# The first block and the value weights of a gated-attention and short-conv layer: low parts on VectorE alone, some weights' high parts on ScalarE

## The chip, the core and the metric

The kernel runs on one core of a Trainium2 chip. The metric is the device time of one launch in microseconds (us). A run is compared by that time; the profile is of one execution and has a span of its own, which is a little shorter than the time of the launch.

## What is computed

The reference is one layer of a streaming encoder trunk, on x of 4096 tokens by 1024 channels in float32:

```
n = RMSNorm(h) * norm_w
z = n @ W_in                 # q, k, v, gate, a_low, and four conv groups, 3600 columns
GLA : 4 heads, chunk-causal gated linear attention with a low-rank decay, RMSNorm per head, SiLU gate
conv: Bg * conv3(Cg * u), SiLU gate
h = h + W_out [GLA ; conv]
h = h + sigmoid(h W_g + b_g) * (p W_ple)
out = RMSNorm(h)
```

All that matters here is the head of it: the norm of the first 512 tokens, and the products of these tokens with the columns of k and a_low (272 of them), of v (512), of q (256) and of the gate (512).

## The kernel before

**Split operands.** TensorE reads float32 operands in the form fp32r. To keep float32 accuracy each operand is split into a high part (the value rounded to fp32r, by ScalarE or GpSimd) and a low part (value minus high part, by VectorE or GpSimd), and each product is three matmuls: high by high, high by low weights, low tokens by high weights (L815, L816 and L823 in `big_tile`). A low part cannot be made before its high part.

**Blocks.** The 4096 tokens are eight blocks of 512. The program has three phases: GLA (eight blocks), a fast matrix product for the conv part and the output projection (`STEPS` of seven products), and the gate phase. For one block, `raw` holds the tokens (eight tiles of 128 channels by 512 tokens), `XH` and `XL` their normalised high and low parts. A GLA block has 14 tiles of 24 matmuls each: in block 0 four ka tiles (128 tokens by 272 columns), four v tiles (128 tokens by 512 columns), two q tiles and four gate tiles.

**The head of the program.** Block 0 is loaded by SyncE's queue in four transfers of 512 KB, then two quarters of the ka weights (`early_ka`), the constants, and the four value tiles (`early_v`). GpSimd's own queue loads the other two quarters of ka into `stage` (L596). ScalarE squares the tokens (L1215), VectorE sums the squares (L1531), TensorE sums over partitions (L846), ScalarE takes the root (L1224). Then VectorE works through the block in two halves of 256 tokens (L1957): reciprocal (L1959), eight normalising instructions (L1964), then low parts k = 3 to 7 (L1970); the low parts k = 0 to 2 of each half are GpSimd's (`lo_of_block_0`, L601). ScalarE makes the high parts of a half as the normalised tiles come (L1500, L1507), and between the halves the high parts of value tiles 1 to 3 (L1503). After the second half VectorE makes the low parts of value tiles 2 and 3 (L1974) and a small one of `wup` (L1978).

**GpSimd's list** (L606) is written out by hand: high and low parts of the four quarters of the ka weights (L636, L638), the three low parts of half A, the loads of the first two of the six q and gate weight tiles (L612, L613), both parts of value tile 0, the three low parts of half B, the low part of value tile 1, then both parts of the six q and gate tiles, and after that twelve `prep_pair` calls that make the weights of the second phase and store them to memory.

**TensorE's waits in block 0.** The first ka tile waits for all four quarters of ka (`ka_tile`, L871), and per k for the high and the low part of half A. The second needs nothing more. The third (tokens 256 to 383) waits per k for half B, the fourth for nothing more. The v tiles wait for all four value tiles (L879, L880), the q and gate tiles for theirs (`weights`, L842). Then, in order: the statistics of block 1 half way through the second q tile (L850, L851; they need `x_split`, L1536), and the decay's sums.

**Block 1's tokens.** SyncE stores the normalised block 0 to memory (L407) once all of it is normalised, and loads block 1 into the same `raw` (L402) once the low parts are done and the store has landed.

Of the kernel before, what the change touches and what calls it, by code (L numbers as in the profile page):

```python
# [28 lines left out]
KT = D_MODEL // P  # L29
HEADS, DK, DV = 4, 64, 128  # L30
QK, RANK, CHUNK = HEADS * DK, 16, 64
KA = QK + RANK
# [2 lines left out]
PLE_K = 2  # L35
UP = 96
EPS = 1e-6
FIRST_LO = 3
V_BY_DVE = 2
HALF_A, HALF_B = slice(0, TB // 2), slice(TB // 2, TB)  # L40
BIG = D_MODEL * 4
ROW = TB * 4
# [1 line left out]
F32 = mybir.dt.float32  # L44
# [52 lines left out]
def build(nc, xb, pb, w_ka, w_in, w_out, w_gate, w_ple, w_up, b_alpha, vectors, masks,  # L97
          out, y_scratch, h_scratch, n_scratch, w_scratch, g_scratch):
    with ExitStack() as ctx:
# [3 lines left out]
        def sem(name):  # L103
            return ctx.enter_context(nc.semaphore(name))
# [107 lines left out]
        stage_loaded = [sem(f"stage_loaded{i}") for i in range(2)]  # L212
        early_loaded = [sem(f"early_loaded{i}") for i in range(6)]
        w_hi = sem("w_hi")
        v_hi = sem("v_hi")
        v_lo = sem("v_lo")
        w_ready = sem("w_ready")
# [121 lines left out]
        def is_first(b):  # L339
            return isinstance(b, int) and b == 0  # L340
# [238 lines left out]
        def _(pool):  # L579
# [15 lines left out]
                src = source(n)  # L595
                pool.dma_start(stage[:, n % 2, 0:src.shape[1]], src).then_inc(stage_loaded[n % 2], 16)  # L596

            def lo_of_block_0(half, hi_done, lo_done):
                for k in range(FIRST_LO):
                    pool.wait_ge(hi_done, k + 1)  # L600
                    pool.tensor_tensor(XL[:, k, half], raw[:, k, half], XH[:, k, half].bitcast(F32),  # L601
                                       ALU.subtract).then_inc(lo_done, 1)

            load(0)
            load(1)
            for n in range(N_W):  # L606
                if W_Q < n < N_W - 1:
                    load(n + 1)
                if n == W_V:
                    lo_of_block_0(HALF_A, first_hi, first_lo)  # L610
                    pool.wait_ge(w_ready, 2)
                    load(W_Q)  # L612
                    load(W_Q + 1)  # L613
                if n == W_V + 1:
                    lo_of_block_0(HALF_B, x_hi, x_lo)
                if W_Q - V_BY_DVE <= n < W_Q:
                    continue
                if 2 <= n < W_Q:
                    source_tile = early_ka[n - 2] if n < W_V else early_v[n - W_V]
                    pool.wait_ge(early_loaded[n - 2], 16)  # L620
                else:
                    source_tile = stage[:, n % 2]
                    pool.wait_ge(stage_loaded[n % 2], 16 * (n // 2 + 1 if n < 2 else n // 2 - 2))
                if n < W_V:
                    hi, lo = KAH[:, 2 * n:2 * n + 2], KAL[:, 2 * n:2 * n + 2]
                    src = source_tile[:, 0:2 * KA].rearrange("p (k c) -> p k c", k=2)
                elif n < W_Q:
                    hi, lo = VH[:, n - W_V], VL[:, n - W_V]
                    src = source_tile.rearrange("p (k c) -> p k c", k=KT)
                else:  # L630
                    hi, lo = QG[:, n - W_Q, 0], QG[:, n - W_Q, 1]
                    src = source_tile.rearrange("p (k c) -> p k c", k=KT)
                if W_V < n < W_Q:
                    pool.wait_ge(v_hi, n - W_V)
                else:
                    pool.tensor_scalar(hi, src, 1.0, 0.0, ALU.mult, ALU.add).then_inc(w_hi, 1)  # L636
                    pool.wait_ge(w_hi, n + 1 if n <= W_V else n - 2)
                pool.tensor_tensor(lo, src, hi.bitcast(F32), ALU.subtract).then_inc(w_ready, 1)  # L638


# [158 lines left out]
        def _(pe):  # L799
            def big_tile(phase, b, i, acc_ap, products, after=None, waits=None):  # L800

                step = 8 * phase + b
                last = i == TILES[phase] - 1
                ahead = phase == GLA and is_first(b) and i == 0
                first = i == (1 if phase == GATE else 2 if phase == GLA and is_first(b) else 0)
                for k in range(KT):
                    hh, lh, hl = products(k)  # L810
                    if ahead:
                        pe.wait_ge(first_hi, k + 1)
                    elif first:
# [53 lines left out]
                return ps[MAIN[i % 3]]  # L867

            def ka_tile(b, t, after=None):
                if is_first(b):  # L870
                    pe.wait_ge(w_ready, W_V)  # L871
                tok = slice(t * P, t * P + P)
                big_tile(GLA, b, ka_place(b, t), main_bank(b, ka_place(b, t))[:, 0:KA],
                         lambda k: ((XH[:, k, tok], KAH[:, k]), (XH[:, k, tok], KAL[:, k]),
                                    (XL[:, k, tok], KAH[:, k])), after)
# [317 lines left out]
        def _(act):  # L1193
# [292 lines left out]
            def out_rms(b):  # L1486
# [2 lines left out]
                nc.scalar.activation(R_out[:], ps[STAT][:], ACT.Sqrt, bias=eps[:], scale=1.0 / D_MODEL).then_inc(  # L1489
                    out_root, 1)  # L1490

            act.wait_ge(memsets, 5)
            nc.scalar.activation(warm[:], eps[:], ACT.Sqrt)
            x_squares(0, range(KT))
            x_rms(0)
            act.wait_ge(consts_loaded, 64)
            nc.scalar.activation(suffix[:], mask[:, 0:P], ACT.Copy).then_inc(suffix_ready, 1)
            for k in range(KT):
                act.wait_ge(first_n, k + 1)
                nc.scalar.activation(XH[:, k, HALF_A], raw[:, k, HALF_A], ACT.Copy).then_inc(first_hi, 1)  # L1500
            for i in range(1, 4):
                act.wait_ge(early_loaded[2 + i], 16)
                nc.scalar.activation(VH[:, i], early_v[i].rearrange("p (k c) -> p k c", k=KT), ACT.Copy).then_inc(  # L1503
                    v_hi, 1)
            for k in range(KT):
                act.wait_ge(n_ready, k + 1)
                nc.scalar.activation(XH[:, k, HALF_B], raw[:, k, HALF_B], ACT.Copy).then_inc(x_hi, 1)  # L1507
            act.wait_ge(up_loaded, 48)
            nc.scalar.activation(wup[:], wup_raw[:], ACT.Copy).then_inc(up_hi, 1)
            over_blocks(act, gla, apart=2)  # L1510
# [7 lines left out]
        def _(dve):  # L1518
# [438 lines left out]
            for half, rstd, n_done, hi_done, lo_done in ((HALF_A, first_rstd, first_n, first_hi, first_lo),  # L1957
                                                         (HALF_B, x_rstd, n_ready, x_hi, x_lo)):
                nc.vector.reciprocal(R[:, half], R[:, half]).then_inc(rstd, 1)  # L1959
                dve.wait_ge(rstd, 1)  # L1960
                for k in range(KT):
                    if k % 2 == 0:
                        dve.wait_ge(raw_loaded[k // 2], 16)
                    nc.vector.scalar_tensor_tensor(out=raw[:, k, half], in0=raw[:, k, half],  # L1964
                                                   scalar=vec[:, V_NORM + k:V_NORM + k + 1], in1=R[:, half],
                                                   op0=ALU.mult, op1=ALU.mult).then_inc(n_done, 1)
                dve.wait_ge(lo_done, FIRST_LO)
                for k in range(FIRST_LO, KT):
                    dve.wait_ge(hi_done, k + 1)
                    nc.vector.tensor_tensor(XL[:, k, half], raw[:, k, half], XH[:, k, half].bitcast(F32),  # L1970
                                            ALU.subtract).then_inc(lo_done, 1)
            for i in range(4 - V_BY_DVE, 4):
                dve.wait_ge(v_hi, i)
                nc.vector.tensor_tensor(VL[:, i], early_v[i].rearrange("p (k c) -> p k c", k=KT),  # L1974
                                        VH[:, i].bitcast(F32), ALU.subtract).then_inc(v_lo, 1)
            dve.wait_ge(up_hi, 1)
# [67 lines left out]
```

## Time and profile before

| | us |
|---|---|
| median of 3 runs | 2061.76 |
| lowest and highest run | 2059.93, 2063.16 |
| time of the profiled execution | 2059.93 |
| span of the profiled execution | 2058.1 |

The profiled execution is also the fastest of the three; 1.8 us of its time lie outside the span. Busy shares of the span are TensorE 97%, VectorE 68%, ScalarE 36%, GpSimd 29%. In the rows below PE is TensorE's matmul, DVE VectorE, ACT ScalarE, POOL GpSimd and SP SyncE; a name like L823 is the line of the kernel. Times of a timeline are counted from the start of the span.

### The profile page before, as it was taken

The page shows a single profiled execution, that of the slowest core. Times are in us where ns is not written, and L with a number is a line of the kernel's source. Part 1 is how long each engine was busy: PE and PEld are TensorE (multiplying, and loading weights), DVE is VectorE, ACT ScalarE, POOL GpSimd, SP SyncE. Part 2 cuts the span into 40 slices and gives each one's busy share as a digit, 9 for nine tenths or more (in the row PEclk, how much of TensorE's full clock was granted, in tenths as well). Part 3 has the DMA queues.
Part 4 walks back from the last instruction along what each step waited for, and adds up shares of the span by engine and source line. Part 5 has one row for each costly group of instructions (what it writes and reads, how often), then busy time and mean ns, then how long its engine had stood idle before and what let it go on. Part 6 is the DMA issues. An engine that isn't in the chain of part 4 may idle for free.

```text
span 2058.1 us, 25907 instructions
## 1 busy us (share of the span) xinstructions
PE 2002.0 (97%) x9730; PEld 1667.3 (81%) x9730; DVE 1394.6 (68%) x1546; ACT 737.7 (36%) x1103; POOL 601.3 (29%) x601
## 2 busy tenths in 40 slices
PE   4999999999999999999999999999999999999997
PEld 3888887888888888888888888878887888888885
DVE  7678989889784785675575576566565456565654
ACT  3454445434533432332332333322222233333331
POOL 7755667667550212112112112155411000000000
PEclk9999999999999999999999999999999999999998
DMA  5354353453544522127312127587577322222111
GB/s 216 120 189 180 143 189 148 173 194 128 204 174 166 202 95 87 46 87 278 138 62 87 56 103 273 176 307 254 212 250 266 122 93 93 92 92 80 68 77 42
DMA packets 82390, 306.72 MB, mean 149 GB/s; under 512 B 10064, under 2 KB 18688, under 8 KB 71808
## 3 DMA queue, kind: packets, MB, share of 16 engines
q1 hardware_dynamic: 53152, 179.17, 23.9%
q0 software_dynamic: 29152, 126.40, 16.9%
q8 instruction: 54, 0.88, 0.2%
q14 instruction: 32, 0.26, 0.0%
HBM read 183.90 MB, written 121.63 MB: 148 GB/s over the span
## 4 chain that ended last, share of the span: by engine, by line
PE 86%; DVE 8%; issue 3%; DMA 1%; POOL 1%; ACT 1%; DVEq 0%; SPq 0%; ACTq 0%; POOLq 0%
PE bank L1067 14%; PE bank L1073 13%; PE bank L1069 13%; PE bank L815 13%; PE bank L823 12%; PE bank L816 12%; PE bank L1155 1%; PE bank L1154 1%; PE bank L1153 1%; PE bank L902 1%; DVE raw L1547 1%; DVE R L1531 1%; DVE XL L1522 1%; DVE rt L1563 1%; PE bank L962 1%
## 5 line engine op out<-in xcount | busy, mean ns | idle before, releaser
L1067 PE MATMUL bank<-XH,WC 128*128 128x512 f32 x1344 | 524.8, 390 | 3.9 <-DVE xt L1865 3.7
L1073 PE MATMUL bank<-XL,WC 128*128 128x512 f32 x1344 | 523.0, 389 | 0.0
L1069 PE MATMUL bank<-XH,WC 128*128 128x512 f32 x1344 | 522.9, 389 | 0.0
L1699 DVE TENSOR_TENSOR XL<-RQ,XH 128x1024 fp32r<-128x1024 f32 x168 | 214.9, 1315 | 230.6 <-ACT XH L1380 229.5
L1067 PEld LDWEIGHTS bank<-XH,WC 128*128 128x128 f32 x1344 | 252.4, 188 | 57.1 <-DVE xt L1865 4.6
L1073 PEld LDWEIGHTS bank<-XL,WC 128*128 128x128 f32 x1344 | 252.3, 188 | 52.6
L1069 PEld LDWEIGHTS bank<-XH,WC 128*128 128x128 f32 x1344 | 252.4, 188 | 51.7
L755 POOL TENSOR_TENSOR RQ<-RQ 128x1024 f32<-128x1024 f32 x48 | 116.2, 2443 | 423.3 <-DVE RQ L1718 404.8
L1380 ACT ACTIVATE XH<-RQ 128x1024 fp32r<-128x1024 f32 x168 | 170.7, 1054 | 164.7 <-PE bank L1073 147.1
L815 PE MATMUL bank<-XH,WG 128*128 128x512 f32 x512 | 199.4, 389 | 0.5 <-issue 0.5
L816 PE MATMUL bank<-XH,WG 128*128 128x512 f32 x512 | 199.3, 389 | 0.0
L823 PE MATMUL bank<-XL,WG 128*128 128x512 f32 x512 | 199.2, 389 | 0.0
L1928 DVE TENSOR_TENSOR t_sb<-gt,bank 128x512 f32<-128x512 f32 x64 | 44.0, 688 | 185.1 <-ACT gt L1477 185.1
L815 PE MATMUL bank<-XH,QG 128*128 128x512 f32 x384 | 152.4, 397 | 0.0
L816 PE MATMUL bank<-XH,QG 128*128 128x512 f32 x384 | 149.8, 390 | 0.0
L823 PE MATMUL bank<-XL,QG 128*128 128x512 f32 x384 | 149.6, 390 | 0.0
L1397 ACT ACTIVATE EA<-bank 128x512 f32<-128x512 f32 x96 | 57.5, 601 | 181.9 <-PE bank L1073 81.2
L815 PEld LDWEIGHTS bank<-XH,WG 128*128 128x128 f32 x512 | 96.1, 188 | 21.0 <-issue 0.9
L823 PEld LDWEIGHTS bank<-XL,WG 128*128 128x128 f32 x512 | 96.1, 188 | 20.1
L816 PEld LDWEIGHTS bank<-XH,WG 128*128 128x128 f32 x512 | 96.1, 188 | 19.9
L661 POOL TENSOR_TENSOR PB<-PB,prep_hi 128x512 f32<-128x512 f32 x84 | 109.4, 1302 | 2.2
L1563 DVE RECIPROCAL rt<-rt 128x512 f32<-128x512 f32 x32 | 107.0, 3344 | 2.5 <-ACT rt L1274 2.5
(191 smaller groups left out, 3481.2 us busy)
## 6 DMA issues: line engine op xcount, KB each, us to landing
WC<-w_scratch SPq DMA_DIRECT2D x21, 2048.0 KB, 8.5
RQ<-n_scratch POOLq DMA_DIRECT2D x32, 1024.0 KB, 5.3
w_scratch<-prep_hi POOLq DMA_DIRECT2D x84, 256.0 KB, 2.3
w_scratch<-PB POOLq DMA_DIRECT2D x84, 256.0 KB, 2.3
raw<-xb_dram SPq DMA_DIRECT2D x32, 512.0 KB, 6.5
n_scratch<-raw SPq DMA_DIRECT2D x8, 2048.0 KB, 7.1
y_scratch<-y_sb SPq DMA_DIRECT2D x64, 256.0 KB, 2.5
RQ<-y_scratch POOLq DMA_DIRECT2D x16, 1024.0 KB, 6.5
```

The lines of the kernel that those rows point to most:

```text
L661: pool.tensor_tensor(PB[:, buf], PB[:, buf], prep_hi[:].bitcast(F32), ALU.subtract).then_inc(prep_done, 1)
L755: pool.tensor_tensor(RQ[:, a, k], RQ[:, Q22, k], RQ[:, b, k], ALU.subtract).then_inc(made, 1)
L815: nc.tensor.matmul(acc_ap, hh[0], hh[1], start=(k == 0), stop=False)
L816: nc.tensor.matmul(acc_ap, lh[0], lh[1], start=False, stop=False)
L823: mm = nc.tensor.matmul(acc_ap, hl[0], hl[1], start=False, stop=(k == KT - 1))
L1067: nc.tensor.matmul(bank[:], WC[:, i, q, 0, k], xh, start=(k == 0 and i in (P1, P2, P5)), stop=False, skip_group_check=True)
L1069: nc.tensor.matmul(bank[:], WC[:, i, q, 1, k], xh, start=False, stop=False, skip_group_check=True)
L1073: mm = nc.tensor.matmul(bank[:], WC[:, i, q, 0, k], xl, start=False, stop=(k == 3), skip_group_check=True)
L1380: nc.scalar.activation(XH[:, slot(s) + 2 * h:slot(s) + 2 * h + 2], RQ[:, OPERAND[i], 2 * h:2 * h + 2], ACT.Copy).then_inc(sx_hi, 1)
L1397: nc.scalar.activation((EB if i == P6 else EA)[:, q], ps[A_BANK[q]][:], ACT.Copy).then_inc(e_copied, 1)
L1563: nc.vector.reciprocal(rt[:], rt[:]).then_inc(head_step, 1)
L1699: nc.vector.tensor_tensor(XL[:, k], RQ[:, OPERAND[s % 7], 2 * h:2 * h + 2], XH[:, k].bitcast(F32), ALU.subtract).then_inc(sx_lo, 1)
```

## The change

GpSimd no longer makes low parts of block 0 nor any part of a value tile. VectorE makes all eight low parts of each half, each two tiles behind the normalising instruction, and the low parts of all four value tiles. ScalarE makes the high parts of two quarters of ka, ahead of the root, and of all four value tiles, two after each half. GpSimd issues its first load only once the second transfer of block 0 has landed, and after ka and two loads it waits until all four value tiles have their low parts before it begins the q and gate tiles. TensorE's wait for ka is now per quarter.

```diff
-FIRST_LO = 3
-V_BY_DVE = 2
+FIRST_AHEAD = 2
+V_BY_DVE = 4
...
-            def lo_of_block_0(half, hi_done, lo_done):
-                for k in range(FIRST_LO):
-                    pool.wait_ge(hi_done, k + 1)
-                    pool.tensor_tensor(XL[:, k, half], raw[:, k, half], XH[:, k, half].bitcast(F32),
-                                       ALU.subtract).then_inc(lo_done, 1)
-
+            pool.wait_ge(raw_loaded[1], 16)
             load(0)
             load(1)
             for n in range(N_W):
                 if W_Q < n < N_W - 1:
                     load(n + 1)
                 if n == W_V:
-                    lo_of_block_0(HALF_A, first_hi, first_lo)
                     pool.wait_ge(w_ready, 2)
                     load(W_Q)
                     load(W_Q + 1)
-                if n == W_V + 1:
-                    lo_of_block_0(HALF_B, x_hi, x_lo)
+                    pool.wait_ge(v_lo, V_BY_DVE)
                 if W_Q - V_BY_DVE <= n < W_Q:
                     continue
...
-                if W_V < n < W_Q:
-                    pool.wait_ge(v_hi, n - W_V)
+                if W_V <= n < W_Q:
+                    pool.wait_ge(v_hi, n - W_V + 1)
+                elif 2 <= n < W_V:
+                    pool.wait_ge(ka_hi, n - 1)
                 else:
                     pool.tensor_scalar(hi, src, 1.0, 0.0, ALU.mult, ALU.add).then_inc(w_hi, 1)
...
                     if ahead:
+                        if k % 2 == 0:
+                            pe.wait_ge(w_ready, k // 2 + 1)
                         pe.wait_ge(first_hi, k + 1)
...
             def ka_tile(b, t, after=None):
-                if is_first(b):
-                    pe.wait_ge(w_ready, W_V)
...
             x_squares(0, range(KT))
+            for i in range(2):
+                act.wait_ge(early_loaded[i], 16)
+                nc.scalar.activation(KAH[:, 2 * i + 4:2 * i + 6],
+                                     early_ka[i][:, 0:2 * KA].rearrange("p (k c) -> p k c", k=2),
+                                     ACT.Copy).then_inc(ka_hi, 1)
             x_rms(0)
...
-            for i in range(1, 4):
-                act.wait_ge(early_loaded[2 + i], 16)
-                nc.scalar.activation(VH[:, i], ...).then_inc(v_hi, 1)
+            value_hi(range(2))
             for k in range(KT):
                 act.wait_ge(n_ready, k + 1)
                 nc.scalar.activation(XH[:, k, HALF_B], raw[:, k, HALF_B], ACT.Copy).then_inc(x_hi, 1)
+            value_hi(range(2, 4))
...
-                for k in range(KT):
-                    if k % 2 == 0:
-                        dve.wait_ge(raw_loaded[k // 2], 16)
-                    nc.vector.scalar_tensor_tensor(out=raw[:, k, half], ...).then_inc(n_done, 1)
-                dve.wait_ge(lo_done, FIRST_LO)
-                for k in range(FIRST_LO, KT):
-                    dve.wait_ge(hi_done, k + 1)
-                    nc.vector.tensor_tensor(XL[:, k, half], ...).then_inc(lo_done, 1)
+                for k in range(KT + FIRST_AHEAD):
+                    if k < KT:
+                        if k % 2 == 0:
+                            dve.wait_ge(raw_loaded[k // 2], 16)
+                        nc.vector.scalar_tensor_tensor(out=raw[:, k, half], ...).then_inc(n_done, 1)
+                    if k >= FIRST_AHEAD:
+                        j = k - FIRST_AHEAD
+                        dve.wait_ge(hi_done, j + 1)
+                        nc.vector.tensor_tensor(XL[:, j, half], ...).then_inc(lo_done, 1)
             for i in range(4 - V_BY_DVE, 4):
-                dve.wait_ge(v_hi, i)
+                dve.wait_ge(v_hi, i + 1)
```

`value_hi` is the loop of L1501 to L1504 as a function of the tiles. The counts of `w_hi` and `w_ready` follow the new division.

## Rows read from the trace of the kernel before

**Rows 1.** The page: busy time of the engines, and SyncE's loads of tokens (KB, us to landing).
```profile
PE 2002.0 (97%) x9730; PEld 1667.3 (81%) x9730; DVE 1394.6 (68%) x1546; ACT 737.7 (36%) x1103; POOL 601.3 (29%) x601
...
raw<-xb_dram SPq DMA_DIRECT2D x32, 512.0 KB, 6.5
```

**Rows 2.** By stretch: us; PE, PEld, DVE, ACT, POOL busy; clock, DMA share, GB/s.
```profile
0.00:50.00 50.00, 21.94 (x93) 18.64 (x94) 38.40 (x38) 18.30 (x38) 36.53 (x39) 0.90 0.58 209
50.00:120.00 70.00, 70.00 (x386) 58.11 (x385) 44.42 (x53) 31.74 (x48) 45.77 (x47) 1.00 0.42 155
```

**Rows 3.** Waits from 0 to 50 us: who for whom, total us, times, longest.
```profile
PE bank L823 <- DVE XL L1970: 10.3, 4, 4.6
```

**Rows 4.** Chain of waits from 10 to 50.7 us: start, us, what.
```profile
10.91 1.65 DVE R L1531
...
12.65 0.95 DVE R L1531
...
16.61 1.76 DVE R L1959
...
18.39 2.89 DVE raw L1964 x5
...
38.01 6.97 DVE XL L1970 x4
```

**Rows 5.** Timeline of VectorE: start, us, instruction.
```profile
27.28 1.42 DVE L1970 TENSOR_TENSOR XL<-raw,XH 128x256 fp32r<-128x256 f32 x4
...
30.39 1.27 DVE L1964 SCALAR_TENSOR_TENSOR raw<-raw,vec,R 128x256 f32<-128x256 f32 x3
...
37.93 2.56 DVE L1970 TENSOR_TENSOR XL<-raw,XH 128x256 fp32r<-128x256 f32 x1
...
45.23 1.21 DVE L1974 TENSOR_TENSOR VL<-early_v,VH 128x1024 fp32r<-128x1024 f32 x1
46.36 1.21 DVE L1974 TENSOR_TENSOR VL<-y_sb,VH 128x1024 fp32r<-128x1024 f32 x1
```

**Rows 6.** Timeline of GpSimd: the last ka part and the first q tile.
```profile
17.50 1.33 POOL L638 TENSOR_TENSOR KAL<-tmp,KAH 128x544 fp32r<-128x544 f32 x1
...
36.53 1.21 POOL L636 TENSOR_SCALAR QG<-stage 128x1024 fp32r<-128x1024 f32 x1
37.82 2.39 POOL L638 TENSOR_TENSOR QG<-stage,QG 128x1024 fp32r<-128x1024 f32 x1
```

**Rows 7.** By stretch, two stretches of unbroken ka matmuls (columns as in rows 2).
```profile
27.80:32.30 4.50, 4.50 (x21) 4.50 (x21) 4.46 (x8) 1.57 (x4) 0.89 (x2) 1.00 0.00 0
32.60:36.00 3.40, 3.38 (x27) 3.15 (x26) 3.40 (x3) 1.24 (x3) 3.40 (x3) 1.00 0.00 0
```

**Rows 8.** Timeline of TensorE: first v tile, first q tile, block 1's statistics.
```profile
50.67 0.39 PE L815 MATMUL bank<-VH,XH 128*128 128x512 f32 x1
...
73.48 0.39 PE L815 MATMUL bank<-XH,QG 128*128 128x512 f32 x1
...
81.65 0.39 PE L850 MATMUL bank<-sum_hi,ones 128*128 128x512 f32 x1
```

**Rows 9.** ScalarE's high parts of half A: ns least, median, most.
```profile
L1500 ACT ACTIVATE XH<-raw x8: 417/418/420, 19.1 to 24.9; 128x256 fp32r<-128x256 f32 x8
```

**Rows 10.** Block 1, timelines of SyncE and VectorE: store, loads, first row sum, split.
```profile
38.09 0.33 SPq L407 DMA_DIRECT2D n_scratch<-raw  x1
45.33 2.09 SPq L402 DMA_DIRECT2D raw<-xb_dram  x4
...
57.68 0.68 DVE L1531 TENSOR_TENSOR R<-sq 128x512 f32<-128x512 f32 x1
...
75.49 1.09 DVE L1536 TENSOR_TENSOR R_lo<-R,sum_hi 128x512 fp32r<-128x512 f32 x1
```

**Rows 11.** By stretch, a block beside GpSimd's work and the first after it.
```profile
437.00:518.00 81.00, 80.23 (x480) 68.63 (x479) 71.41 (x70) 39.02 (x65) 56.82 (x67) 1.00 0.45 167
...
599.00:680.00 81.00, 79.85 (x473) 68.03 (x473) 45.13 (x53) 30.30 (x49) 9.69 (x8) 1.00 0.56 222
```

More of the change, by code:

```diff
@@ L214, in build @@
         w_hi = sem("w_hi")
+        ka_hi = sem("ka_hi")
         v_hi = sem("v_hi")
@@ L632, in _ @@
                     src = source_tile.rearrange("p (k c) -> p k c", k=KT)
-                if W_V < n < W_Q:
-                    pool.wait_ge(v_hi, n - W_V)
+                if W_V <= n < W_Q:
+                    pool.wait_ge(v_hi, n - W_V + 1)
+                elif 2 <= n < W_V:
+                    pool.wait_ge(ka_hi, n - 1)
                 else:
                     pool.tensor_scalar(hi, src, 1.0, 0.0, ALU.mult, ALU.add).then_inc(w_hi, 1)
-                    pool.wait_ge(w_hi, n + 1 if n <= W_V else n - 2)
+                    pool.wait_ge(w_hi, n + 1 if n < W_V else n - W_Q + 3)
                 pool.tensor_tensor(lo, src, hi.bitcast(F32), ALU.subtract).then_inc(w_ready, 1)
@@ L1490, in out_rms, with value_hi @@
                     out_root, 1)
+            def value_hi(tiles):
+                for i in tiles:
+                    act.wait_ge(early_loaded[2 + i], 16)
+                    nc.scalar.activation(VH[:, i], early_v[i].rearrange("p (k c) -> p k c", k=KT), ACT.Copy).then_inc(
+                        v_hi, 1)
             act.wait_ge(memsets, 5)
@@ L1500, in _ @@
                 nc.scalar.activation(XH[:, k, HALF_A], raw[:, k, HALF_A], ACT.Copy).then_inc(first_hi, 1)
-            for i in range(1, 4):
-                act.wait_ge(early_loaded[2 + i], 16)
-                nc.scalar.activation(VH[:, i], early_v[i].rearrange("p (k c) -> p k c", k=KT), ACT.Copy).then_inc(
-                    v_hi, 1)
+            value_hi(range(2))
             for k in range(KT):
@@ L1960, in _ @@
                 dve.wait_ge(rstd, 1)
-                for k in range(KT):
-                    if k % 2 == 0:
-                        dve.wait_ge(raw_loaded[k // 2], 16)
-                    nc.vector.scalar_tensor_tensor(out=raw[:, k, half], in0=raw[:, k, half],
-                                                   scalar=vec[:, V_NORM + k:V_NORM + k + 1], in1=R[:, half],
-                                                   op0=ALU.mult, op1=ALU.mult).then_inc(n_done, 1)
-                dve.wait_ge(lo_done, FIRST_LO)
-                for k in range(FIRST_LO, KT):
-                    dve.wait_ge(hi_done, k + 1)
-                    nc.vector.tensor_tensor(XL[:, k, half], raw[:, k, half], XH[:, k, half].bitcast(F32),
-                                            ALU.subtract).then_inc(lo_done, 1)
+                for k in range(KT + FIRST_AHEAD):
+                    if k < KT:
+                        if k % 2 == 0:
+                            dve.wait_ge(raw_loaded[k // 2], 16)
+                        nc.vector.scalar_tensor_tensor(out=raw[:, k, half], in0=raw[:, k, half],
+                                                       scalar=vec[:, V_NORM + k:V_NORM + k + 1], in1=R[:, half],
+                                                       op0=ALU.mult, op1=ALU.mult).then_inc(n_done, 1)
+                    if k >= FIRST_AHEAD:
+                        j = k - FIRST_AHEAD
+                        dve.wait_ge(hi_done, j + 1)
+                        nc.vector.tensor_tensor(XL[:, j, half], raw[:, j, half], XH[:, j, half].bitcast(F32),
+                                                ALU.subtract).then_inc(lo_done, 1)
             for i in range(4 - V_BY_DVE, 4):
-                dve.wait_ge(v_hi, i)
+                dve.wait_ge(v_hi, i + 1)
                 nc.vector.tensor_tensor(VL[:, i], early_v[i].rearrange("p (k c) -> p k c", k=KT),
```

## The prediction

> **What bounds the kernel now.** I read the page first: TensorE is busy for 2002.0 us [rows 1] of a span of 2058.1, so the whole gets shorter only where TensorE stands still. The busy time by stretch shows where that is: of its 56 idle us, 28 lie in the first 50 us, and none in the 70 us that follow [rows 2]. The table of waits names the owner of a good part: TensorE waits 10.3 us, in four pieces of up to 4.6, for low parts that VectorE makes [rows 3]. The chain of waits shows that from the row sums to 44.98 us the path is nearly all VectorE [rows 4]. From there TensorE finishes the ka tiles on its own and takes up the v tiles at 50.67 us [rows 8]; after that it does not pause for 70 us. So 50.67 is the number to move: an earlier start of the v tiles is a gain to the end, unless something behind it becomes late.
>
> **Why VectorE is slow there.** The same low part of 256 columns takes two very different times. Four in a row took 1.42 us, (1.42 - 0.41) / 3 = 0.34 us from start to start; one beside GpSimd's subtraction took 2.56 us, and ended at 40.49, just behind GpSimd's, which ended at 40.21 [rows 5, 6]. A normalising instruction takes 0.40 us ((1.27 - 0.48) / 2) when quiet [rows 5]. In half B eight of these and five low parts, 8 x 0.40 + 5 x 0.34 = 4.9 us of work, lay between 30.39 and 44.98. The other ten us are waiting for GpSimd.
>
> **The change, part by part.**
>
> *Start of half A.* It stood at 18.39: the row sums ended at 13.60, and TensorE's mean, the root and a reciprocal of 1.76 came behind [rows 4]. GpSimd comes to ka later, since its loads wait for a transfer, but does less there: four subtractions and two copies, where it had four and four; its last subtraction ended at 18.83 [rows 6]. The last sums took 1.65 and 0.95 us where a quiet one takes 0.68 [rows 4, 10]; undisturbed, they bring the half forward by 1.3. If GpSimd's work falls on the first normalising instructions instead, they lose about 1.0. I take 18.4 plus 0.5. ScalarE's two extra copies lie between its last square and the root, over two us in which it waits for TensorE's mean: nothing. GpSimd's two weight loads move to right behind ka, and nobody waits for them before 37 us. TensorE's wait per quarter costs nothing, as the first quarter is ready when half A starts.
>
> *Two halves.* Each is now eight pairs of one normalising and one low-part instruction: 8 x (0.40 + 0.34) = 5.9 us. That is the lower bound; the upper is full durations without overlap, 0.48 + 0.41 = 0.89 a pair, 7.1 us. I take 5.9: a low part follows its tile by three instructions (1.1 us), and ScalarE needs 0.42 us for the high part [rows 9]. With a reciprocal of 1.8 between the halves: 18.9 + 5.9 + 1.8 + 5.9 = 32.5, in place of 45.3.
>
> Here a rule speaks against the change. The Trainium skill, page "VectorE: DVE Perf Modes", section "The DRAIN you can't avoid", says that the next instruction starts only when the pipe of the one before is empty. By it a half would be 7.1 us, and the v tiles 2.4 us later than in my sum. The trace, with 0.34 us between starts of instructions of 0.41, does not agree.
>
> *Value tiles.* VectorE makes four in place of two, at 1.13 us from start to start [rows 5]: 4.5 us. ScalarE has the high parts of tiles 0 and 1 before half B's, and 2 and 3 behind the last of half B's, while VectorE is at 0 and 1. All low parts are there at 37.0, and the v tiles can start at **37.1**.
>
> *TensorE must keep up.* It runs at two levels: 4.5 us hold 20 ka matmuls of 272 columns, 0.225 us each, which is 1.2 GHz, and a little later 3.4 us hold 27, 0.126 each, which is 2.4 GHz; the clock column shows 1.00 for both, so the pace decides [rows 7]. In the first ka tile TensorE needs 3 x 0.225 = 0.68 us per k and VectorE gives one per 0.74; the tile ends at about 25.2. Before, the level rose after this 4.5 us stretch of unbroken work, so I take the high one from 25 on: second tile 24 x 0.126 = 3.0, done at 28.2; the third follows half B to 32.9; the fourth is done at 35.9. That is before 37.1: VectorE is the bound.
>
> The v tiles thus start 50.7 - 37.1 = **13.6 us earlier**.
>
> *GpSimd after that.* It waits for the value tiles until 37.0. Before, it began its first q tile at 36.53 [rows 6], so its list stays where it was. The first tile is ready at 40.7; TensorE wanted it at 73.48 [rows 8], now at 59.9. Even at 5 us each the sixth is ready at 67, and TensorE is there five tiles of 5.4 us after the first, at 87. Nothing waits, and what lies behind on its queue does not move.
>
> *Block 1.* SyncE's store of block 0 was issued at 38.09 and the loads 7.2 us later [rows 10]. Now the last tile is normalised at about 31.5, so the loads go out at 38.7 instead of 45.33: only 6.6 us earlier, not 13.6. VectorE's first row sum of block 1 stood at 57.68 [rows 10] and is wanted at 44.1. It needs the first of four transfers, which have a median of 6.5 us to landing [rows 1], and 1.2 us of squares: 46.4 at most, late by 0 to 2.3; I take 1. From there the chain to the split of the sums now runs wholly beside GpSimd's q and gate tiles, where before its later part met a quiet GpSimd. The split ended at 76.58 and TensorE asked for it at 81.65 [rows 10, 8]: 5.1 us of slack. One to two more waits of 2.4 us can fall in it. Between 0 and 2.5 us come through; I take 0.6.
>
> *Later blocks.* GpSimd's preparation ends when it did, and TensorE is ahead by 13.6 us, so that much more of the blocks runs beside it. VectorE is busy 71.4 of 81 us in such a block, 45.1 in the first after it, and TensorE lacks 0.8 and 1.2 us in these two [rows 11]. I take 0.5 us, bounds 0 and 3.5.
>
> **The sum.** 13.6 - 0.6 - 0.5 = 12.5 us. Against the profiled execution's 2059.93 this is 2047.4. That one was the fastest of three; against their median of 2061.76 it is 2049.3. I say **2049.0**.
>
> **The rivals.**
>
> *TensorE stays at, or falls back to, 1.2 GHz.* In the third ka tile it has 3 x 0.126 = 0.38 us of work per 0.74. If it is slow throughout, three tiles take 5.4 us each and the v tiles start at 25.2 + 16.2 = 41.4; if it falls in the third tile, the fourth ends at 38.3 and the first v tiles are slow too, 2 to 3 us more. Either way the gain is near 9.5, less 1.1: 2053.4. For it: it was at this level for much of the ka tiles. Against: there it had stood still for up to 4.6 us [rows 3]. The Trainium skill, page "TensorE: Matmul & The Clock Gate", section "What's actually happening", says that the low level is the default and that the level follows how busy the engine has recently been. By it this rival is open.
>
> *Block 1's sums are late.* The waits pile up and the loads come late: 4 us lost, 2052.8. For it: loads only 6.6 us earlier. Against: 5.1 us of slack.
>
> *The lead is given back in the GLA blocks.* VectorE, slowed by GpSimd, sets their pace and eats 10 us or more: 2059 to 2062. For it: 71.4 of 81. Against: TensorE lacks about 1 us a block, so it sets the pace.
>
> *Slower: the long VectorE instructions are not GpSimd's doing.* Then the 13 instructions of half B at (44.98 - 30.39) / 13 = 1.12 us are what they cost, and VectorE gets six more and two value tiles at 1.2: 6.7 + 2.4 = 9.1 us on top of 47.57, when it was done with them. The v tiles start at 56.8, 6.1 us later: 2067.9. It decides from a pair of 1.84 us upwards, where the start passes 54.8. Against: 0.34 and 0.40 us in the quiet rows [rows 5].
>
> **How the numbers follow.** Forecast 0.62, clock 0.14, late sums 0.14, lead given back 0.06, slower 0.04. The range goes from a half A 1.3 us earlier than 18.4 with nothing lost behind (v tiles at 35.3, 2046.4; 1.4 for the scatter of the runs) to the clock rival with 1.6 us lost behind it: **2045 to 2055**; the second and third case lie in it. A measurement here can tell 0.2%, 4.1 us, from no change. The first three cases are faster by more, of the fourth a part: faster 0.93, same 0.04, slower 0.03.
>
> **What would show it.** After: pairs at 0.74 us and no VectorE instruction over 1.3 us between 20 and 37 us except reciprocals; last low part of half B at 32.5; first v matmul at 37; ka matmuls at 0.126 us in the second and fourth tile; GpSimd idle from 19 to 37; no TensorE gap at block 1's statistics. I am wrong if the v tiles start after 41, or if TensorE's idle time after 50 us grows by more than 3 us.

## The result, and the profile after

The changed kernel takes **2051.95 us** (median of six runs, 2045.27 to 2053.48), against 2062.37 for the kernel before, timed beside it (six runs, 2059.93 to 2064.28): 0.9945 of its time, with a 95% interval of 0.9932 to 0.9957. That is 10.4 us or 0.55% faster. The forecast was 2049.0, range 2045 to 2055. The profiled execution took 2053.48, the longest of its six; that of before, 2059.93, was the shortest of its own. Those two differ by 6.45 us only, so the size of the gain is taken from the medians, and not from the two profiles.

The page of the kernel after, its span and the busy time of its engines (as rows 1):

```profile
span 2051.7 us, 25908 instructions
PE 2001.9 (98%) x9730; PEld 1664.6 (81%) x9730; DVE 1387.2 (68%) x1554; ACT 738.3 (36%) x1106; POOL 578.8 (28%) x590
```

TensorE does the same work [rows 1]. Its idle time fell from 56.1 to 49.8 us, which is the whole difference of the two spans.

The busy time by stretch, kernel after: the first 50 us and the next 70 (as rows 2), and two stretches of ka matmuls (as rows 7), from the second and the third ka tile.

```profile
0.00:50.00 50.00, 30.52 (x158) 25.39 (x159) 32.05 (x54) 25.79 (x52) 21.37 (x28) 1.00 0.66 239
50.00:120.00 70.00, 68.94 (x412) 58.42 (x411) 57.56 (x52) 29.93 (x47) 44.95 (x46) 1.00 0.45 162
24.50:28.30 3.80, 3.80 (x32) 3.80 (x32) 3.76 (x7) 2.62 (x6) 0.00 (x0) 1.00 0.00 0
29.30:32.00 2.70, 2.44 (x13) 1.78 (x14) 2.70 (x8) 1.76 (x5) 0.00 (x0) 1.00 0.01 6
```

TensorE has 158 matmuls in the first 50 us, where it had 93 [rows 2]. In the stretch of the third row it starts one per 0.126 us (from 24.58 to 28.24 us, 29 steps), which is 2.4 GHz.

The waits from 0 to 50 us, kernel after: who for whom, total us, times, longest.

```profile
POOL QG L633 <- DVE VL L1982: 16.9, 1, 16.9
PE bank L845 <- DMA bias<-b_alpha_dram: 12.8, 1, 12.8
...
PE bank L814 <- ACT a_rep L1235: 1.6, 1, 1.6
...
PEld bank L822 <- DVE XL L1978: 1.2, 4, 0.3
```

The 10.3 us that TensorE waited for low parts [rows 3] are down to four waits of 0.3 on its loads of weights. GpSimd's 16.9 us are its wait for the value tiles, in which it stands aside. Two rows are new: TensorE's mean (the sum over partitions) waits for the last constant to land, and a ka tile waits 1.6 us for ScalarE.

The chain of waits of the kernel after, from 10 to 37 us (as rows 4):

```profile
12.84 2.06 PE bank L845 x2
14.92 0.70 ACT R L1221
15.71 1.76 DVE R L1966
17.49 2.31 DVE raw L1972 x3
...
26.16 1.28 DVE raw L1972 x3
...
31.12 0.42 ACT XH L1513
31.54 1.90 ACT VH L1493 x2
33.44 0.31 ACT wup L1516
33.74 0.27 ACT ka_sb L1234
34.01 0.14 ACT a_rep L1235
34.20 0.39 PE bank L814
```

Up to 31 us it is VectorE's, as before. Then it passes to ScalarE and TensorE, where the one of before had 6.97 us of low parts on VectorE [rows 4].

Timelines of the kernel after, VectorE, GpSimd, SyncE and TensorE: start, us, instruction; in brackets the idle time before it, and what ended it.

```profile
17.49 1.91 DVE L1972 SCALAR_TENSOR_TENSOR raw<-raw,vec,R 128x256 f32<-128x256 f32 x2
20.06 0.47 DVE L1972 SCALAR_TENSOR_TENSOR raw<-raw,vec,R 128x256 f32<-128x256 f32 x1
20.45 0.41 DVE L1978 TENSOR_TENSOR XL<-raw,XH 128x256 fp32r<-128x256 f32 x1
20.79 0.47 DVE L1972 SCALAR_TENSOR_TENSOR raw<-raw,vec,R 128x256 f32<-128x256 f32 x1
...
32.01 3.48 DVE L1982 TENSOR_TENSOR VL<-early_v,VH 128x1024 fp32r<-128x1024 f32 x3
35.42 1.21 DVE L1982 TENSOR_TENSOR VL<-y_sb,VH 128x1024 fp32r<-128x1024 f32 x1
44.29 1.19 DVE L1538 TENSOR_TENSOR R<-sq 128x512 f32<-128x512 f32 x1
```
```profile
17.40 1.33 POOL L635 TENSOR_TENSOR KAL<-tmp,KAH 128x544 fp32r<-128x544 f32 x1
...
36.73 1.27 POOL L633 TENSOR_SCALAR QG<-stage 128x1024 fp32r<-128x1024 f32 x1 [16.91 <-DVE VL L1982]
```
```profile
37.50 2.61 SPq L404 DMA_DIRECT2D raw<-xb_dram  x4
```
```profile
37.32 0.40 PE L814 MATMUL bank<-VH,XH 128*128 128x512 f32 x1
...
665.10 0.39 PE L1064 MATMUL bank<-XH,WC 128*128 128x512 f32 x1
```

From 20.06 to 20.45 to 20.79: a normalising instruction occupies VectorE for 0.39 us and a low part for 0.34, now in turns. The v tiles start at **37.32**, where they started at 50.67 [rows 8]: 13.35 us earlier. The last row is the first matmul of the stage behind the GLA blocks; in the kernel before it stood at 676.70. The lead there is 11.6 us, and at the end of the span 6.4.

So two questions stand. Which part of the change brought the 13.35 us? And where did nearly seven of them go, in stages that the change does not touch?

### The profile page after: what moved, and what is told of

Read it like the earlier page. It is cut to its first block, busy times and chain, and to the rows that moved or that the text cites. A ratio compares the mean times of both kernels' runs of the same rounds, so it can differ in the third digit from the quotient of the medians.

```text
span 2051.7 us, 25908 instructions
## 1 busy us (share of the span) xinstructions
PE 2001.9 (98%) x9730; PEld 1664.6 (81%) x9730; DVE 1387.2 (68%) x1554; ACT 738.3 (36%) x1106; POOL 578.8 (28%) x590
## 3 DMA queue, kind: packets, MB, share of 16 engines
q0 software_dynamic: 29152, 126.40, 16.9%
## 4 chain that ended last, share of the span: by engine, by line
PE 84%; DVE 8%; issue 3%; DMA 2%; ACT 1%; POOL 1%; SPq 0%; DVEq 0%; ACTq 0%; POOLq 0%
PE bank L1064 13%; PE bank L1070 13%; PE bank L1066 13%; PE bank L814 12%; PE bank L822 12%; PE bank L815 12%; PE bank L1152 1%; PE bank L1151 1%; PE bank L1150 1%; DVE raw L1554 1%; PE bank L899 1%; DVE XL L1529 1%; DVE rt L1570 1%; PE bank L959 1%; DVE hist L1638 1%
## 5 line engine op out<-in xcount | busy, mean ns | idle before, releaser
L1706 DVE TENSOR_TENSOR XL<-RQ,XH 128x1024 fp32r<-128x1024 f32 x168 | 210.4, 1288 | 235.3 <-ACT XH L1377 234.4
```

The costliest lines, as they stand in the source:

```text
L1706: nc.vector.tensor_tensor(XL[:, k], RQ[:, OPERAND[s % 7], 2 * h:2 * h + 2], XH[:, k].bitcast(F32), ALU.subtract).then_inc(sx_lo, 1)
```

## The experiments

All were timed beside the kernel before, in three groups (experiments 1 to 4, 5 to 8, 9 to 12), in which its median was 2062.65, 2063.31 and 2061.37. Each ratio below is to that kernel, with its 95% interval. "v" is the start of the first v matmul, before at 50.67.

**1. The changed kernel again**, without an edit.

> The changed kernel as it is, to see what of its profile repeats. My theory: the first v matmul again at 37.3 us, within 0.3, since all before it is fixed work of VectorE; the lead over the kernel before is 12 to 13 us at the end of the first phase; what the first profiled execution lost in the output projection (waits for x tiles) differs from execution to execution, so the time is 10 to 13 us below the kernel before, ratio 0.9937 to 0.9952. Rival: the loss in the output projection is a lasting effect of the change; then the waits of TensorE between 1340 and 1600 us are again over 8 us, and the time is 10 us or less below.

2051.61 us (2050.01 to 2053.39), 0.9945 [0.9931, 0.9958]; v at 37.32 again. The gain is reproduced, and so is its size. The stage behind the GLA blocks did not differ as expected: from its first matmul to the last of the program it took 1373.0 us, after 1373.2 in the first profile. The rival's sign, over 8 us of waits for x tiles, did not come either (5.9).

**2. GpSimd doesn't stand aside**, all else as in the changed kernel.

```
-                    pool.wait_ge(v_lo, V_BY_DVE)
```

> The changed kernel, but GpSimd does not wait for the value tiles' low parts before it begins the q and gate tiles, so it works beside VectorE from about 23 us. Theory (GpSimd's two-input instructions hold VectorE up): the pieces of VectorE's work from 23 us on take up to 2.5 us each instead of 0.34 to 0.48, VectorE's rate becomes one or two instructions per GpSimd instruction, the last value tile is ready after 45 us and the v tiles start at 45 to 52 us; the time comes back by 6 to 12 us, to 2057 to 2063. Rival (the division of the work and its order make the gain): v tiles still start before 39 us and the time stays within 2 us of the changed kernel.

2066.07 us (2060.92 to 2071.08), 1.0014 [1.0003, 1.0025]: not merely the gain lost, but as slow as before or a little slower. v at 57.31, later than before. The loss was underestimated: v was expected at 52 at most, the time at 2063. Timelines of this kernel, VectorE and then GpSimd:

```profile
33.01 2.58 DVE L1977 TENSOR_TENSOR XL<-raw,XH 128x256 fp32r<-128x256 f32 x1
35.52 0.47 DVE L1971 SCALAR_TENSOR_TENSOR raw<-raw,vec,R 128x256 f32<-128x256 f32 x1
35.91 1.67 DVE L1977 TENSOR_TENSOR XL<-raw,XH 128x256 fp32r<-128x256 f32 x1
37.50 2.57 DVE L1971 SCALAR_TENSOR_TENSOR raw<-raw,vec,R 128x256 f32<-128x256 f32 x1
39.99 0.41 DVE L1977 TENSOR_TENSOR XL<-raw,XH 128x256 fp32r<-128x256 f32 x1
```
```profile
32.89 2.42 POOL L634 TENSOR_TENSOR QG<-stage,QG 128x1024 fp32r<-128x1024 f32 x1
35.61 0.59 POOL L598 DMA_DIRECT2D stage<-w_in_dram  x1 [0.30 <-POOL QG L634]
36.24 1.06 POOL L632 TENSOR_SCALAR QG<-stage 128x1024 fp32r<-128x1024 f32 x1
37.38 2.40 POOL L634 TENSOR_TENSOR QG<-stage,QG 128x1024 fp32r<-128x1024 f32 x1
```

These rows show the contention most plainly. VectorE's three long instructions end at 35.59, 37.58 and 40.07; GpSimd's end at 35.31, 37.30 and 39.78. Each of VectorE's ends 0.28 or 0.29 us behind GpSimd's, whatever its own length, and the two between them that met no arithmetic of GpSimd's took 0.47 and 0.41. Without the wait, the new division gives VectorE more two-input work in just the stretch in which GpSimd holds it up. The wait is worth 14 us (2066.07 - 2051.6).

**3. GpSimd stands aside from the q tiles on, and nothing else is changed**: the division of before, with the same wait.

```
+                if n == W_Q:
+                    pool.wait_ge(v_lo, V_BY_DVE)
```

> The kernel before, with one thing added: GpSimd waits for VectorE's two value tiles before it begins the q and gate tiles. Theory: half B's low parts k = 3 to 7, which took 2.56 us beside the first q tiles, take 0.34; the v tiles start some 6 us earlier than 50.7, at 43 to 46 us, and the time is 4 to 7 us below the kernel before. Rival (GpSimd is not the cause): no change in VectorE's durations, and the v tiles at 50 us or later.

2057.14 us (2050.67 to 2061.49), 0.9972 [0.9959, 0.9984]: half of the gain. v at 42.94, 7.7 us earlier; 43 to 46 was expected, and 4 to 7 us of gain. VectorE of this kernel, the low parts of half B, alone at last:

```profile
37.69 1.75 DVE L1972 TENSOR_TENSOR XL<-raw,XH 128x256 fp32r<-128x256 f32 x5
```

Five took 1.75 us, where the chain of before has 6.97 for the last four [rows 4]. They ended at 39.44 in place of 45.30, 5.9 us earlier. The other 1.9 us come with TensorE's clock: it made its last ka tile at one matmul per 0.126 us, where in the kernel before it made most of it at 0.225 (granted clock 0.50 from 45 to 49 us), behind its waits for low parts. The normalising of half B still lies beside GpSimd's low parts and value tile (eight in 6.82 us). The wait and the division need each other: the wait alone brings 5.5 us, the division alone loses 3.4, and the two together bring 11.0.

**4. No interleaving**: each half normalised whole, then its low parts.

```
-FIRST_AHEAD = 2
+FIRST_AHEAD = 8
```

> The changed kernel, but in each half VectorE makes all eight normalised tiles first and then the eight low parts. Theory: VectorE's total is the same, 5.9 us per half, and the last value tile is ready at the same 36.6 us; what changes is TensorE, which cannot use the first half's low parts before 22 us and has less time for its four ka tiles: at 1.2 GHz for longer, it ends the fourth at 38 to 41 us, so the v tiles start 1 to 3 us later and the time is up by as much. Rival: the interleaving is worth nothing, v tiles at 37.3.

2051.85 us (2049.93 to 2052.21), 0.9944 [0.9928, 0.996]; v at 36.70. The expectation (v 1 to 3 us later) failed, and its rival held. The order of VectorE's instructions is worth nothing in time: its work has the same sum in either order, and its last value tile's low part ended at 36.59, against 36.63.

**5. The kernel before again**, for its landmarks.

> The kernel before as it is, for a second profile of it. Question: the changed kernel's profiles lost 5 us of their lead in the output projection, measured against a profile of before that was among the fastest of its runs. Theory: that loss is the scatter of the kernel before; in this profile TensorE's waits for x tiles between 1300 and 1620 us are 5 to 6 us in place of 3.7, and the time is 2061 to 2064. Rival: the kernel before always has 3.7 us there, so the change costs 2 us or more in a stage that it does not touch.

2062.24 us (2058.17 to 2065.25), 0.9993 [0.9982, 1.0005]; v at 50.24. The waits for x tiles were 4.1 us, nearer to the rival's 3.7 than to the 5 to 6 expected. The profile is used below, where the later stages are compared.

**6. The last two ka low parts on VectorE too, and the first ka tile's bank emptied early.** In the changed kernel VectorE is done with the row sums at 11.93 us and stands idle until 15.71, while GpSimd's last two ka subtractions run on into the first normalising instructions (1.91 us for two above). So VectorE makes them, behind the row sums; TensorE waits for them on a semaphore of their own. And ScalarE empties the first tile's bank ahead of half B's high parts.

```
+            for i in range(2):
+                dve.wait_ge(ka_hi, i + 1)
+                nc.vector.tensor_tensor(KAL[:, 2 * i + 4:2 * i + 6],
...
+            ka_out(0, 0)
```

> The changed kernel with two more moves: the low parts of the last two quarters of ka go from GpSimd to VectorE, which stands idle between the last row sum (11.9 us) and the reciprocal (15.7), and ScalarE empties the first ka tile's bank after value tiles 0 and 1, ahead of half B, so that the fourth ka tile does not wait. Theory: GpSimd is done with ka at 16.2 us and no longer holds up the first normalising instruction (1.51 us in place of 0.47), the gap of 1.6 us before the fourth ka tile goes, the v tiles start at 35.6 to 36.0 and the time falls by 1.3 to 1.7 us to about 2050. Rival: something else is late by then and the v tiles stay at 37.3, or TensorE waits later; no gain.

2045.07 us (2042.62 to 2052.14), **0.992** [0.9899, 0.994]; v at 36.21. VectorE of this kernel:

```profile
11.99 0.72 DVE L1969 TENSOR_TENSOR KAL<-L,KAH 128x544 fp32r<-128x544 f32 x1
...
17.99 0.48 DVE L1983 SCALAR_TENSOR_TENSOR raw<-raw,vec,R 128x256 f32<-128x256 f32 x1
```

The first normalising instruction is back at 0.48 us. The v tiles start 1.1 us earlier; 1.3 to 1.7 were expected, of the time as well. But the median falls by 6.5 us. The six times fall apart: 2042.62 to 2045.52 (four), and 2051.13 and 2052.14.

**7. GpSimd's first loads aren't held back.**

```
-            pool.wait_ge(raw_loaded[1], 16)
```

> The changed kernel, but GpSimd issues its first two loads at once, as before. Theory: its ka work starts at 9.6 us and slows the last row sums, so half A starts at 18.3 instead of 17.5; but then GpSimd is done with ka before that and the first normalising instruction is not held up, so the v tiles start within 0.4 us of 37.3 and the time is the same within 1 us: the held load wins 0.9 us and gives it back. Rival: the held load is worth its 0.9 us.

2051.73 us (2050.46 to 2056.36), 0.9947 [0.993, 0.9963]; v at 38.45. VectorE is done with the value tiles at 36.26, 0.37 earlier; TensorE is later instead: behind the same wait of 1.57 us for ScalarE it falls to 1.2 GHz in the fourth ka tile, with a matmul per 0.225 us from 34.30 to 37.46 (granted clock 0.79 from 32 to 40 us), where the changed kernel kept 2.4 GHz. v was expected within 0.4 us of 37.3. In time it makes no difference.

**8. GpSimd keeps two of the four value tiles**, behind the wait.

```
-V_BY_DVE = 4
+V_BY_DVE = 2
```

> The changed kernel, but only value tiles 2 and 3 get their low parts on VectorE; GpSimd waits for those and then makes the low parts of 0 and 1 at 2.4 us each before the q tiles. Theory: VectorE is done with tile 3 at 34.8, GpSimd with tile 1 at 39.7, the v tiles start at 39.9, 2.6 us later, and the time is 2 to 3 us above the changed kernel. Rival: the division of the value tiles does not matter, as something else sets 37.3.

2052.56 us (2052.16 to 2054.69), 0.9949 [0.9929, 0.9969]; v at 39.92, 2.6 us later, as expected. Of the 2 to 3 us expected in the time about 1 is seen, less than the runs scatter.

**9. The mean no longer waits for the constants**, on top of experiment 6.

```
-            pe.wait_ge(consts_loaded, 64)
             x_stats(0)
+            pe.wait_ge(consts_loaded, 64)
```

> The kernel of the run ka_on_vector, and TensorE's wait for the constants stands behind its first mean instead of ahead of it. In the changed kernel the row sums ended at 11.93 us but the mean began at 12.84, when the last constant had landed. Theory: the mean begins at 12.1, half A 0.6 to 0.9 us earlier than in ka_on_vector, the v tiles at 35.3 to 35.6, and with the same blocks behind it the time is 0.5 to 1 us lower. Rival: what lies behind the v tiles decides by more than that; then the time goes another way than the start, by up to 5 us.

2046.19 us (2041.95 to 2049.3), 0.9927 [0.9914, 0.994]; v at 35.20. TensorE of this kernel:

```profile
12.32 2.04 PE L850 MATMUL bank<-R,ones 128*128 128x512 f32 x2 [12.32 <-DVE R L1544]
```

The mean now follows the row sums, and v comes 1.0 us earlier than in experiment 6; the times cannot tell them apart, though 0.5 to 1 us less was expected.

**10 and 11. The two parts of experiment 6, each alone**: VectorE's two ka low parts; the early emptying.

> The changed kernel with only the first of the two moves of ka_on_vector: the low parts of two quarters of ka on VectorE; ScalarE empties the first ka bank where it did. Theory: the fourth ka tile still waits, for 1 us or more, so the v tiles start at 36.2 to 37.0; the stretch from the first v matmul to the first product of the next phase is 623 us as in ka_on_vector if the phase between GpSimd and VectorE makes it, 628 as in the changed kernel if the early emptying does.

> The changed kernel with only the second move: ScalarE empties the first ka tile's bank ahead of half B. Theory: the gap of 1.6 us before the fourth ka tile goes, but VectorE's last value tile still ends at 36.6, so the v tiles start at 36.7, 0.6 us earlier, and the time is 0 to 1 us lower. Rival: this move makes the blocks behind it shorter too, and the time is 3 us or more lower.

2046.53 us (2044.85 to 2054.07), 0.9937 [0.9922, 0.9951], v at 36.60; and 2051.23 us (2050.62 to 2051.47), 0.995 [0.9937, 0.9963], v at 36.87. They move v by 0.7 and 0.45 us. The early emptying brings no more than that. The ka parts seem to bring 5 us.

**12. Experiment 6 again**, to see whether its 6.5 us belong to the kernel or to the execution.

> The kernel of ka_on_vector once more, since its six times lay in two groups, four of 2042.6 to 2045.5 and two of 2051 to 2052. Theory: the first v matmul repeats at 36.2 and the stretch behind it at 623 us; the second phase and what follows takes 1368 to 1373 us and is what differs between the groups. Rival: the blocks differ from execution to execution too.

2047.64 us (2040.62 to 2052.91), 0.9925 [0.9907, 0.9943]: three times near 2042.7, three near 2051.6. The two profiles of this one kernel came from the two groups. TensorE's landmarks, first v matmul and first matmul behind the GLA blocks, of the execution of 2042.62 us and then of that of 2052.91:

```profile
36.21 0.47 PE L819 MATMUL bank<-VH,XH 128*128 128x512 f32 x1 [1.08 <-issue]
...
658.62 0.39 PE L1069 MATMUL bank<-XH,WC 128*128 128x512 f32 x1
```
```profile
35.77 0.47 PE L819 MATMUL bank<-VH,XH 128*128 128x512 f32 x1 [1.09 <-issue]
...
663.84 0.39 PE L1069 MATMUL bank<-XH,WC 128*128 128x512 f32 x1
```

The GLA blocks took 622.4 us in one and 628.1 in the other, the rest to the last matmul 1368.8 and 1373.5. The early stage was even a little quicker in the slower one. The expectation (623 us of blocks again) failed; its rival held. So some 10 us come and go with the execution, in stages with the same instructions.

The edit still matters for it. Of the 23 executions of kernels with the two ka low parts on VectorE (experiments 6, 9, 10, 12), 15 took less than 2047 us; of the 32 of the changed kernel and of experiments 1, 4, 7, 8 and 11, which also stand aside and don't have them, one did. So this move makes the quicker group likelier, and the 5 us of experiment 10 are mostly that, since its own effect on v is 0.7. Why it does is not shown.

**Where the later microseconds go.** Part of it can be read in all fourteen profiles. In the output projection TensorE waits two or three times for VectorE's x tiles. The wait for them from 1300 to 1620 us, in before and after:

```profile
PE bank L1067 <- DVE xt L1865: 3.7, 2, 2.2
```
```profile
PE bank L1064 <- DVE xt L1872: 5.8, 3, 3.1
```

In after, ahead of the longer one, VectorE first stands still for 4.95 us until GpSimd has made its additions of 1024 columns (two in 4.74 us, which had waited for a load). Then two additions of VectorE's of the same size take 5.38 us, beside GpSimd's and what it does behind them; a subtraction of that size took 1.21 us alone. That looks like the same contention, but no run varied it, so it is not shown. Here are the stretches behind the longest of these waits, in before and after:

```profile
1367.00:1371.00 4.00, 1.87 (x9) 1.22 (x7) 4.00 (x4) 1.61 (x2) 3.63 (x5) 1.00 0.90 274
1371.00:1375.00 4.00, 3.94 (x17) 3.27 (x18) 4.00 (x6) 1.11 (x2) 2.25 (x2) 1.00 0.97 342
```
```profile
1357.00:1361.00 4.00, 0.90 (x4) 0.44 (x4) 4.00 (x4) 1.90 (x2) 3.63 (x5) 1.00 0.85 288
1361.00:1365.00 4.00, 4.00 (x12) 3.09 (x12) 4.00 (x5) 0.22 (x1) 1.95 (x2) 0.57 0.97 341
```

In the second row of each TensorE works without a break: 17 matmuls in 4 us at a granted clock of 1.00, 12 at 0.57. Behind its wait it fell to 1.2 GHz, and the profile of after has the same a second time, at 1573 us. Before has it at neither place. Set against the length of the last part (first matmul behind the blocks to the last one), this accounts for nearly all of it:

| profile | x waits, us | falls of the clock | last part, us | 1368.0 + (waits - 3.7) + 1.4 x falls |
|---|---|---|---|---|
| before | 3.7 | 0 | 1368.0 | 1368.0 |
| experiment 6 | 4.4 | 0 | 1368.8 | 1368.7 |
| before again (5) | 4.1 | 1 | 1369.6 | 1369.8 |
| loads not held (7) | 5.7 | 0 | 1370.3 | 1370.0 |
| GpSimd doesn't stand aside (2) | 5.1 | 2 | 1372.4 | 1372.2 |
| after | 5.8 | 2 | 1373.2 | 1372.9 |
| experiment 12 | 5.8 | 2 | 1373.5 | 1372.9 |

The 1.4 us for one fall is fitted to these rows, not measured by itself. The seven profiles left out agree with the column within 0.5 us. No edit was aimed at these waits or at the clock, and experiments 6 and 12, 4.7 us apart in the fourth column, are the same kernel.

The other part is the GLA blocks. From the first v matmul to their end they took 621.7 to 622.4 us in four profiles (experiments 2, 6, 9 and 10) and 625.9 to 628.8 in the other ten. For the one kernel of experiments 6 and 12 the place can be read. Block 2's v tiles start at 177.7 us in experiment 6 and at 183.1 in 12. This is TensorE from 98 to 184 us in the two, and one row of 12's timeline:

```profile
98.00:184.00 86.00, 85.57 (x507) 72.83 (x507) 74.61 (x77) 41.46 (x70) 51.99 (x61) 1.00 0.49 183
```
```profile
98.00:184.00 86.00, 82.25 (x477) 69.35 (x476) 77.02 (x70) 38.79 (x66) 53.91 (x63) 0.98 0.47 175
```
```profile
141.58 0.48 PE L854 MATMUL bank<-sum_hi,ones 128*128 128x512 f32 x1 [1.82 <-DVE hsq_lo L1566]
```

TensorE stands still for 3.3 us more in experiment 12, and behind this wait for VectorE's low parts of squares it falls to 1.2 GHz (granted clock 0.72 from 140 to 146 us). With 1.4 us for the fall that is 4.7 us; the blocks of the two differ by 5.7. In the profile of after the waits for the same low parts from 37.5 to 680 us are:

```profile
PE bank L849 <- DVE hsq_lo L1560: 4.6, 5, 1.8
```

VectorE works beside GpSimd there, so that the phase between the two can differ; but no run here fixes that phase, and why one execution falls on one side is not shown.

## Why the prediction was right, point by point

**The mechanism** was the right one. Experiment 2 shows it directly, and it rules out the rival in which long VectorE instructions are not GpSimd's doing: with GpSimd still they took 0.34 and 0.40 us from start to start, in after too. By the Trainium skill's rule that the next instruction waits until the pipe is empty ("VectorE: DVE Perf Modes", "The DRAIN you can't avoid"), as the prediction read it, a half would have taken 7.1 us. Half B took 5.9, from 26.16 to the last low part at 32.09. The prediction left out what the same section adds, that an instruction which is not held back behind the one in front starts earlier. With that the trace agrees (0.34 us between starts of instructions of 0.41).

**The start of the v tiles** was forecast at 37.1 and came at 37.32, but two errors nearly cancelled in it, so that its closeness is partly luck.
- *Start of half A*: 18.4 plus 0.5 was forecast, with a gain of 1.3 in the row sums or a loss of 1.0 in the first instructions. Both came. The sums ended at 11.93 where they ended at 13.60. Of those 1.7 us, 0.9 reached half A, which began at 17.49. The other 0.8 went to a wait that the prediction had not seen: the mean waits for the last constant, and began at 12.84. That was hidden as long as the sums were later. Then 1.0 went to GpSimd's last ka subtraction, which ended at 18.73: the first normalising instruction lasted until 19.00, 1.51 us in place of 0.48. Half B's last low part then came at 32.09 (forecast 32.5), the last value tile's at 36.63 (37.0).
- *TensorE must keep up*: this step failed. Its fourth ka tile was to end at 35.9 and ended at 37.3. It uses the bank of the first, which ScalarE empties, and ScalarE did the high parts of two value tiles and one weight first. The tile stood still for 1.57 us, from 32.6 to 34.20. "ScalarE's two extra copies: nothing" was right; the order of its other work, behind half B, was not followed through. TensorE and VectorE thus ended within 0.7 us of each other, which is why experiments 4, 10 and 11 moved the start by 0.7 us or less.

**The clock rival** did not come about in the changed kernel's profile. TensorE kept 2.4 GHz through the third ka tile, where half B fed it three matmuls, 0.38 us of work, per 0.73. In experiment 7 it did: the fourth tile ran at 1.2 GHz behind the same 1.57 us wait, and v came 1.1 us later. So it is a matter of the execution that the changed kernel's profile shows no fall there.

**Block 1**: its first row sum came at 44.29 (44.1 wanted), SyncE's loads at 37.50 (forecast 38.7). TensorE took up the split sums at 68.26 without a wait; 0.8 us went to a wait for one of the block's low parts, against the 0.6 forecast. GpSimd's q tiles began at 36.73 (36.53 before), as forecast. Of the later blocks, 0.5 us was forecast; before to after the GLA blocks grew by 1.8, block 1 included, between two profiles that need not be of the same group.

**The missing term** is the scatter behind the blocks. The prediction has nothing for the last part, which was 5.2 us longer in the profile of after than in that of before: 2.1 of waits for x tiles, and 2.8 of lower clock by the fit above. Between medians it is less. A gain of 12.5 us was summed and 10.4 measured. "TensorE's idle time after 50 us grows by more than 3 us" was a sign of being wrong; it grew by 2.3.

**The rival of a lead given back** is thus a part right in size, though not in place. The contention did not eat the lead in the GLA blocks (1.8 us of 13.35).

**The best version** is that of experiments 6 and 9: 0.992 to 0.993 of the time before, in all three timings. Against the changed kernel's medians that is 4 to 7 us, of which 1 to 2 us can be seen in the start of the v tiles; the rest is that more of its executions fall in the quicker group (11 of 17 under 2047 us). Whether that share lasts is not shown.

## What to carry to other kernels

When VectorE's instructions of one shape take either 0.4 or 2.6 us, look at what GpSimd does in the same microseconds: giving VectorE more work and making GpSimd wait beat sharing it, and neither half of that pair was enough alone. Before costing an earlier start, list what else the freed engine waits for (a constant, a bank that a third engine empties), for each was hidden until then. And when two medians differ by more than the start that was moved, profile one kernel twice before believing it.

## What the runs showed of the hardware

- VectorE's two-input instructions of 256 columns end 0.28 us after the instruction of GpSimd's that they meet, also behind one of GpSimd's with a single input (36.24 to 37.30 us in experiment 2). A reciprocal of 256 columns took 1.75 us beside GpSimd's subtractions (at 15.71 in after) and 1.74 with GpSimd still (at 24.39).
- In the output projection a wait of 2 to 3 us was followed in some executions by some 4 us at 1.2 GHz, and in others of the same kernel by none. In the GLA blocks falls came behind waits of 1.7 and 1.8 us (experiments 3 and 12). In the head, the same wait of 1.57 us in front of the fourth ka tile was followed by a fall in experiment 7 and by none in after. The Trainium skill ("TensorE: Matmul & The Clock Gate", "What's actually happening") has the level follow how busy the engine has recently been; these rows agree as far as it goes, and don't show what decides between two executions.
- One kernel on one core, on one chip, gave times of 2040.62 and 2052.91, in two groups. In the two profiles of it most of the difference lies in TensorE's waits for VectorE, and in the clock behind them.
